# A vector engine's place for splitting weights: before or behind the residual sum of an expert block

## The chip, the cores and the metric

One core of one Trainium2 chip runs the whole program. The metric is the device time of one execution in microseconds; a kernel's time is the median of its runs. The engines are TensorE (PE), VectorE (DVE), ScalarE (ACT), GpSimd (POOL) and SyncE (SP); each works through its own instruction stream in order, and they wait for each other by semaphores.

## The reference

A decoder layer on x of 2048 tokens by 1024 channels, all float32: a norm with conditioning, an RG-LRU token mixer, a second norm, a mixture of 16 experts of width 256 with the two best of one group of four for each token, and a final norm. The part that matters here:

```
x = x + g1[:, None, :] * y
hn = modulate(rmsnorm(x, norm2_g[i]), sh2, sc2)
x = x + g2[:, None, :] * grouped_moe(hn, ...)      # act = silu(hn @ w_gate) * (hn @ w_up) * gate; out = act @ w_down
return rmsnorm(x, final_norm_g)
```

## The kernel before, in words

The program has three stretches: norm and transpose, then the mixer (to about 590 us of the trace), then output projection and routing (to about 820 us), then the experts. Routing writes each token's normed row twice into slots sorted by expert (`hn_slots`), with a record of where its sum is to go, and its residual row (`x_slots`). Slots are cut into blocks of 128 rows; with these inputs there are 39 blocks for 16 experts. Most experts have two or three blocks, one has a single one.

A float32 matmul is made of three passes in a faster format: a value is split into a high half (a rounded copy, made by ScalarE) and a low half (value minus high, made by VectorE), and hi x hi, hi x lo and lo x hi are added. Gate and up weights of an expert are split this way in three parts: part 0 and 1 of 1536 columns, part 2 of 1024. Part 3 is the down weight, which is only copied (2048 columns). SP loads the raw parts; it reloads a raw buffer once the low half (for part 3 the copy) has been made.

The loop over blocks is written out by hand in each engine's stream, with the stages of several blocks interleaved:

- TensorE (`expert_tensor`, L1567), iteration i: `gate_up(i + 2)`, 24 matmuls over eight k; in front of k = 0, 3 and 6 it waits for the low half of part 0, 1 and 2 (L1590). In front of k = 6 and behind that wait it turns the activations of the block before (`turn_act`, L1602, L1605). Then `turn(i + 3)`, the transpose of the gathered rows (L1574), and `down(i + 1)` (L1608, matmuls L1618), which waits for `ah_ready` and for `acc_ready` of the block before.
- ScalarE (`expert_scalar`), iteration i: `load_x(i + 1)` (issues the load of the residual rows, L1400, waits for `acc_ready`), `square(i)` (L1441, waits for the sum of block i), `high_a(i + 1)` (L1412, the activations that `down(i + 1)` needs), `tanh(i + 2)`, `high_x(i + 3)`, `scale_row(i)` (L1432), `high_w(i + 2)` (L1414, copies at L1425).
- VectorE (`expert_vector`, L1494), iteration i: `act_product(i + 2)` (L1505, L1508), `low_x(i + 3)` (L1515), `y_scaled(i + 1)` (L1520, waits for the down of block i + 1), `accumulate(i + 1)` (L1530 copies an index, L1531 makes the sum `e_ab`; they wait for the scatter of the block before, `acc_out`), then the low halves `low_w` (L1288, L1296).
- GpSimd (`expert_gpsimd`), iteration i: `weigh(i)` (L1323, L1325), `scatter_out(i)` (L1313), `scatter_acc(i + 1)` (L1306, writes the sum back to `x_slots`, waits for `acc_ready`), `root(i + 1)` (L1333 to L1341).

Which weights are converted beside which block is in a table, `tab["convert"]`, read by `convert_word` (L1282): beside an expert's first block parts 0 and 1 of the next expert are made, beside its second block part 2 (and ScalarE copies part 3), and beside a block that is its expert's only one all of them. ScalarE's `high_w` waits until the downs of the expert before are done (`d_mm`), since they use the same half of the buffer. `low_w` waits for each high half by `hi_done`:

```
for q in ((0, 1), (2,))[part]:
    dve.wait_ge(w["hi_done"], NQ * e + (q + 1))
```

Of the kernel before, what the change touches and what calls it, by code (L numbers as in the profile page):

```python
# [1217 lines left out]
def experts(nc, ctx, sem, cst, io, tab, w, dr, g2row, out):  # L1218


    if True:
# [60 lines left out]
        def convert_word(eng, b):  # L1282

            v = eng.value_load(tab["convert"][0:1, ds(b, 1)], min_val=128 + 4, max_val=128 * MAXB + 4 * E + 3)
            expert = (v >> 2) & 31
            return ((v >> 1) & 1, v & 1), expert, (expert & 1) * DOWN, v >> 7

        def low_w(dve, word):  # L1288
            dues, e, off, before = word
            for part in range(2):  # L1290
                with dve.If(dues[part] == 1):
                    for q in ((0, 1), (2,))[part]:
                        dve.wait_ge(w["hi_done"], NQ * e + (q + 1))
                        dve.nop(nofuse=True)
                        cols = ds(off + QAT[q], QAT[q + 1] - QAT[q])
                        nc.vector.tensor_tensor(w["lo"][:, cols], raw1[q][:], w["hi"][:, cols].bitcast(F32),  # L1296
                                                ALU.subtract).then_inc(w["lo_done"][q % 2], 1)
# [196 lines left out]
        def expert_vector(dve):  # L1494
            def low_first(q):
                dve.wait_ge(w["hi_done"], q + 1)
                wcols = slice(QAT[q], QAT[q + 1])
                nc.vector.tensor_tensor(w["lo"][:, wcols], raw0[q][:], w["hi"][:, wcols].bitcast(F32),
                                        ALU.subtract).then_inc(w["lo_done"][q % 2], 1)

            def act_product(b):
                if isinstance(b, int) and b == 0:
                    dve.wait_ge(rec_in, 16 * LEAD)
                dve.wait_ge(th_ready, b + 1)
                nc.vector.scalar_tensor_tensor(th[:], th[:], 1.0, gu[:, 0:FE], ALU.add, ALU.mult).then_inc(tmp_ready, 1)  # L1505
                dve.wait_ge(tmp_ready, b + 1)
                dve.nop(nofuse=True)
                nc.vector.scalar_tensor_tensor(av[:], th[:], recs[:].bitcast(F32)[:, ds(b, 1), 2], gu[:, FE:2 * FE],  # L1508
                                               ALU.mult, ALU.mult).then_inc(av_ready, 1)

            def low_x(b):
                for h in range(2):
                    cols = slice(h * HX, (h + 1) * HX)
                    dve.wait_ge(xh_ready, 2 * b + h + 1)
                    nc.vector.tensor_tensor(xl[:, cols], tp[:, cols], xh[:, cols].bitcast(F32), ALU.subtract)\  # L1515
                        .then_inc(xl_ready, 1)

            def y_scaled(b):
                dve.wait_ge(d_mm, b + 1)
                nc.vector.tensor_tensor(pd[:], pd[:], g2row[:], ALU.mult).then_inc(y_ready, 1)  # L1520

            def accumulate(b, first=False):
                dve.wait_ge(y_ready, b + 1)
                dve.wait_ge(xa_in, (b + 1) * 16)
                if not first:
                    dve.wait_ge(squared, b)
                    dve.wait_ge(scaled_row, b)
                    dve.wait_ge(acc_out, b * 16)
                dve.nop(nofuse=True)
                nc.vector.tensor_copy(idx_a[:], recs[:, ds(b, 1), 0]).then_inc(idx_a_ready, 1)  # L1530
                nc.vector.tensor_tensor(ab, pd[:], xa[:], ALU.add).then_inc(acc_ready, 1)  # L1531

            low_x(0)
            low_first(2)
            nless = blocks_less(dve)
            low = lambda b: low_w(dve, convert_word(dve, b))
            act_product(0)
            low_x(1)
            dve.wait_ge(w["lo_done"][0], 2)
            dve.wait_ge(w["hi_done"], NQ)  # L1540
            low(0)
            act_product(1)
            low_x(2)
            y_scaled(0)
            accumulate(0, True)
            low(1)
            for b in range(2):
                act_product(b + 2)
                low_x(b + 3)
                y_scaled(b + 1)  # L1550
                accumulate(b + 1)
                low(b + 2)
            with dve.Fori(2, nless) as i:
                act_product(i + 2)
                low_x(i + 3)
                word = convert_word(dve, i + 2)
                y_scaled(i + 1)
                accumulate(i + 1)
                low_w(dve, word)
            act_product(nless + 2)  # L1560
            y_scaled(nless + 1)
            accumulate(nless + 1)
            low(nless + 2)
            y_scaled(nless + 2)
            accumulate(nless + 2)

        def expert_tensor(pe):  # L1567
# [69 lines left out]
            down(nless + 2)  # L1637

        return expert_sync, expert_scalar, expert_vector, expert_gpsimd, expert_tensor


# [101 lines left out]
```

## Time and profile before

| | us |
|---|---|
| median of 3 runs | 1295.15 |
| lowest, highest | 1294.07, 1295.36 |
| the profiled execution | 1300.12 |
| its span | 1298.5 |
| granted TensorE clock over the span | 0.945 of full |

| engine | busy us | share of the span |
|---|---|---|
| PE | 1097.5 | 85% |
| DVE | 792.0 | 61% |
| ACT | 621.8 | 48% |
| POOL | 632.7 | 49% |

Times in the trace are counted from the start of the span. A line of a timeline has start, duration, engine, source line, operation, output <- inputs, and in brackets the idle time of the engine ahead of it with what ended it. A matmul's end is modelled. PEclk is the mean granted clock of TensorE: 1.00 is 2.4 GHz and 0.50 is 1.2 GHz. "issue" is idle time for which the profile shows no other engine as its cause.

### The profile page before, as it was taken

The page shows a single profiled execution, that of the slowest core. Times are in us where ns is not written, and L with a number is a line of the kernel's source. Part 1 is how long each engine was busy: PE and PEld are TensorE (multiplying, and loading weights), DVE is VectorE, ACT ScalarE, POOL GpSimd, SP SyncE. Part 2 cuts the span into 40 slices and gives each one's busy share as a digit, 9 for nine tenths or more (in the row PEclk, how much of TensorE's full clock was granted, in tenths as well). Part 3 has the DMA queues.
Part 4 walks back from the last instruction along what each step waited for, and adds up shares of the span by engine and source line. Part 5 has one row for each costly group of instructions (what it writes and reads, how often), then busy time and mean ns, then how long its engine had stood idle before and what let it go on. Part 6 is the DMA issues. An engine that isn't in the chain of part 4 may idle for free. (4 is left out here: it accounts for less than half of the span.)

```text
span 1298.5 us, 18937 instructions
## 1 busy us (share of the span) xinstructions
PE 1097.5 (85%) x4704; PEld 837.5 (64%) x4705; DVE 792.0 (61%) x1193; ACT 621.8 (48%) x851; POOL 632.7 (49%) x681
## 2 busy tenths in 40 slices
PE   1358999999999999189999991799789899999991
PEld 0246787787787787178888871576566566666660
DVE  6894557666676684445667768365456555556541
ACT  1464676667667765423222212255555645555541
POOL 0465537246255270012566667055546556656663
PEclk9998999999999999589999995799898999999996
DMA  8445153344334412462354627866677876776741
GB/s 307 162 114 186 52 180 104 111 133 148 98 117 149 130 49 96 180 229 89 133 194 186 225 116 259 276 223 229 224 260 247 276 280 233 249 243 231 247 132 65
DMA packets 142583, 232.55 MB, mean 179 GB/s; under 512 B 32576, under 2 KB 100160, under 8 KB 141904
## 3 DMA queue, kind: packets, MB, share of 16 engines
q1 hardware_dynamic: 101776, 128.10, 29.9%
q0 software_dynamic: 23632, 62.49, 13.5%
q10 hardware_dynamic: 17136, 41.51, 9.9%
q8 instruction: 17, 0.28, 0.1%
q14 instruction: 22, 0.18, 0.0%
HBM read 177.43 MB, written 91.31 MB: 207 GB/s over the span
## 5 line engine op out<-in xcount | busy, mean ns | idle before, releaser
L1618 PE MATMUL po<-w_dn,e_ah 128*128 (+1 forms) x312 | 146.9, 615 | 19.9 <-ACT e_ah L1412 11.9
L1597 PE MATMUL pl<-w_hi,e_xh 128*128 (+1 forms) x312 | 142.8, 458 | 9.6 <-DVE w_lo L1296 5.1
L1165 PE MATMUL po<-wo_hi,b_yh 128*128 128x512 f32 x256 | 105.6, 412 | 27.6 <-DVE wo_lo L979 27.6
L1599 PE MATMUL pl<-w_hi,e_xl 128*128 (+1 forms) x312 | 126.0, 404 | 0.0
L1598 PE MATMUL pl<-w_lo,e_xh 128*128 (+1 forms) x312 | 125.5, 402 | 0.0
L1325 POOL TENSOR_TENSOR e_ob<-e_obs,e_fg 128x1024 f32<-128x1024 f32 x39 | 93.5, 2397 | 56.7 <-ACT e_obs L1432 56.7
L543 DVE SCALAR_TENSOR_TENSOR XB<-xu,conv_w,XB 128x512 f32<-128x512 f32 x96 | 91.4, 952 | 43.0 <-ACT XB L413 39.3
L1618 PEld LDWEIGHTS po<-w_dn,e_ah 128*128 128x128 f32 x312 | 58.4, 197 | 81.4 <-issue 81.4
L636 PE MATMUL px<-hT_hi,wx_hi 128*128 128x512 f32 x256 | 102.0, 398 | 5.1 <-DVE wx_lo L477 5.1
L636 PE MATMUL pg<-hT_hi,wg_hi 128*128 128x512 f32 x256 | 104.2, 407 | 0.0
L1167 PE MATMUL po<-wo_hi,b_yl 128*128 128x512 f32 x256 | 102.3, 400 | 0.0
L1166 PE MATMUL po<-wo_lo,b_yh 128*128 128x512 f32 x256 | 102.1, 399 | 0.0
L637 PE MATMUL px<-hT_lo,wx_hi 128*128 128x512 f32 x256 | 101.8, 398 | 0.0
L638 PE MATMUL px<-hT_hi,wx_lo 128*128 128x512 f32 x256 | 101.8, 398 | 0.0
L638 PE MATMUL pg<-hT_hi,wg_lo 128*128 128x512 f32 x256 | 101.1, 395 | 0.0
L637 PE MATMUL pg<-hT_lo,wg_hi 128*128 128x512 f32 x256 | 101.1, 395 | 0.0
L1441 ACT ACTIVATE e_sq<-e_ab 128x1025 f32<-128x1025 f32 x39 | 41.4, 1062 | 102.3 <-DVE e_ab L1531 95.4
L612 POOL TENSOR_SCALAR macc<-stg,cond 128x512 f32<-128x512 f32 x8 | 11.3, 1407 | 155.3 <-PE pmod L659 149.9
L618 POOL TENSOR_TENSOR macc<-macc,mtmp 128x512 f32<-128x512 f32 x56 | 84.3, 1505 | 4.7
L1597 PEld LDWEIGHTS pl<-w_hi,e_xh 128*128 128x128 f32 x312 | 60.8, 195 | 31.7 <-issue 21.4
L1408 ACT ACTIVATE e_xh<-b_pt 128x512 fp32r<-128x512 f32 x78 | 42.3, 595 | 78.0 <-issue 49.5
L1306 POOL DMA_INDIRECT x_slots<-e_ab,e_idx_a x38 | 44.9, 1183 | 62.6 <-DVE e_ab L1531 55.0
(266 smaller groups left out, 2661.8 us busy)
## 6 DMA issues: line engine op xcount, KB each, us to landing
e_xg<-hn_slots ACTq DMA_DIRECT2D x40, 512.0 KB
e_xa<-x_slots ACTq DMA_DIRECT2D x39, 512.0 KB
stg<-in_ada_w_dram POOLq DMA_DIRECT2D x32, 512.0 KB, 4.2
w_raw<-in_moe_w_down_dram SPq DMA_DIRECT2D x16, 1024.0 KB
w_raw<-in_moe_w_gate_dram SPq DMA_DIRECT2D x32, 384.0 KB
w_raw<-in_moe_w_up_dram SPq DMA_DIRECT2D x32, 384.0 KB
n_ada<-in_ada_w_dram SPq DMA_DIRECT2D x16, 512.0 KB, 5.0
n_x<-in_x_dram SPq DMA_DIRECT2D x16, 512.0 KB, 3.3
```

Of the source, the lines that this page charges most:

```text
L543: nc.vector.scalar_tensor_tensor(xb, xu[:, n, w:w + NB], cw[:, ds(j, 1), w], xb, ALU.mult, ALU.add).then_inc(done, 1)
L636: nc.tensor.matmul(dst[:], whi[br][:, k], hT_hi[:, k, cols], start=(k == 0), stop=False)
L637: nc.tensor.matmul(dst[:], whi[br][:, k], hT_lo[:, k, cols], start=False, stop=False)
L638: last = nc.tensor.matmul(dst[:], wlo[br][:, k], hT_hi[:, k, cols], start=False, stop=(k == KD - 1))
L1165: nc.tensor.matmul(po[u][:, hcols], yh[u][:, tok], wo_hi[:, k, hcols], start=(k == 0), stop=False)
L1166: nc.tensor.matmul(po[u][:, hcols], yh[u][:, tok], wo_lo[:, k, hcols], start=False, stop=False)
L1167: last = nc.tensor.matmul(po[u][:, hcols], yl[u][:, tok], wo_hi[:, k, hcols], start=False, stop=(k == KD - 1))
L1325: nc.gpsimd.tensor_tensor(ob[:], obs[:], fg[:], ALU.mult).then_inc(out_ready, 1)
L1597: nc.tensor.matmul(gu[:], xh[:, tok], hi, start=(k == 0), stop=False)
L1598: nc.tensor.matmul(gu[:], xh[:, tok], lo, start=False, stop=False)
L1599: last = nc.tensor.matmul(gu[:], xl[:, tok], hi, start=False, stop=(k == KD - 1))
L1618: last = nc.tensor.matmul(dst, ah[:, k * P:(k + 1) * P], rows, start=(k == 0), stop=(k == KF - 1))
```

## The change

VectorE's low halves of a block's weights are moved from behind `accumulate` to in front of it, behind `y_scaled`. In the two blocks written out ahead of the loop, in the loop and behind it the order becomes `y_scaled`, low halves, `accumulate`. `low(0)` and `low(1)` keep their places. Nothing else changes; the instructions are the same.

```diff
@@ -1548,19 +1548,19 @@
                 act_product(b + 2)
                 low_x(b + 3)
                 y_scaled(b + 1)
+                low(b + 2)
                 accumulate(b + 1)
-                low(b + 2)
             with dve.Fori(2, nless) as i:
                 act_product(i + 2)
                 low_x(i + 3)
                 word = convert_word(dve, i + 2)
                 y_scaled(i + 1)
+                low_w(dve, word)
                 accumulate(i + 1)
-                low_w(dve, word)
             act_product(nless + 2)
             y_scaled(nless + 1)
+            low(nless + 2)
             accumulate(nless + 1)
-            low(nless + 2)
             y_scaled(nless + 2)
             accumulate(nless + 2)
```

## Rows read from the trace of the kernel before

**Rows 1.** Windows: span, each engine's busy us, PEclk, DMA share, GB/s; the loop
```profile
844.00:1275.00 431.00, 391.90 (x1556) 267.61 (x1554) 237.37 (x304) 229.93 (x319) 250.49 (x303) 0.96 0.69 234
```

**Rows 2.** Waits of PE, 844 to 1275 us: waiting, releaser, total us, times, longest
```profile
PE prank L1605 <- DVE w_lo L1296: 13.9, 6, 3.5
PE po L1618 <- ACT e_ah L1412: 11.9, 4, 5.4
PE po L1618 <- issue: 7.9, 6, 1.8
```

**Rows 3.** Timeline of PE: the first down, two late in the loop, the last
```profile
840.31 3.60 PE L1618 MATMUL po<-w_dn,e_ah 128*128 128x512 f32 x8
...
1240.39 3.60 PE L1618 MATMUL po<-w_dn,e_ah 128*128 x8
...
1250.41 3.60 PE L1618 MATMUL po<-w_dn,e_ah 128*128 x8
...
1269.73 5.15 PE L1618 MATMUL po<-w_dn,e_ah 128*128 x8 [5.41 <-ACT e_ah L1412]
```

**Rows 4.** Groups of DVE by line and shape, 848 to 1275 us: the low halves
```profile
L1296 DVE TENSOR_TENSOR w_lo<-w_raw,w_hi 128x1536 f32 x28 | 47.8, 1750 | 0.1
...
L1296 DVE TENSOR_TENSOR w_lo<-w_raw,w_hi 128x1024 f32 x15 | 18.2, 1216 | 0.4 <-issue 0.4
```

**Rows 5.** Timeline, one step with parts 0 and 1, 1043.94 to 1053.93 us
```profile
1043.94 1.23 DVE L1520 TENSOR_TENSOR po<-po,g2row 128x1024 f32<-128x1024 f32 x1 [0.38 <-PE po L1618]
...
1045.79 1.21 DVE L1531 TENSOR_TENSOR e_ab<-po,e_xa 128x1024 f32<-128x1024 f32 x1
1046.92 3.42 DVE L1296 TENSOR_TENSOR w_lo<-w_raw,w_hi 128x1536 f32 x2
...
1044.34 2.87 ACT L1425 ACTIVATE w_hi<-w_raw 128x1536 f32 x2 [0.58 <-PE po L1618]
...
1050.33 3.60 PE L1618 MATMUL po<-w_dn,e_ah 128*128 x8
```

**Rows 6.** Timeline, the step behind it, from its scatter to its down
```profile
1049.94 1.24 POOL L1306 DMA_INDIRECT x_slots<-e_ab,e_idx_a  x1 [0.30 <-issue]
...
1053.97 1.23 DVE L1520 TENSOR_TENSOR po<-po,g2row 128x1024 f32<-128x1024 f32 x1 [0.28 <-PE po L1618]
1059.39 0.15 DVE L1530 COPY e_idx_a<-e_recs 128x1 int32 x1 [4.19 <-DMA x_slots<-e_ab,e_idx_a]
...
1063.21 5.39 PE L1618 MATMUL po<-w_dn,e_ah 128*128 x8 [2.50 <-ACT e_ah L1412]
```

**Rows 7.** Timeline, one step with part 2, 1177.49 to 1184.98 us
```profile
1177.49 1.23 DVE L1520 TENSOR_TENSOR po<-po,g2row 128x1024 f32<-128x1024 f32 x1 [0.35 <-PE po L1618]
1181.82 0.15 DVE L1530 COPY e_idx_a<-e_recs 128x1 int32 x1 [3.10 <-DMA x_slots<-e_ab,e_idx_a]
...
1183.02 1.22 DVE L1296 TENSOR_TENSOR w_lo<-w_raw,w_hi 128x1024 f32 x1
...
1178.19 1.06 ACT L1425 ACTIVATE w_hi<-w_raw 128x1024 f32 x1 [0.44 <-issue]
...
1184.29 0.69 PE L1605 MATMUL prank<-ident,e_av 128*128 128x128 f32 x2 [2.75 <-DVE w_lo L1296]
```

**Rows 8.** Windows behind two waits of PE (of 3.48 and 2.50 us)
```profile
967.10:970.50 3.40, 3.40 (x18) 2.62 (x19) 0.89 (x2) 1.44 (x4) 2.28 (x6) 1.00 0.90 244
...
1063.21:1068.60 5.39, 5.39 (x9) 2.37 (x10) 2.10 (x4) 2.10 (x3) 3.42 (x6) 0.68 0.89 295
```

**Rows 9.** Timeline of POOL: output scatter without and with low halves on DVE beside it
```profile
1035.10 1.09 POOL L1313 DMA_INDIRECT out_dram<-e_ob,e_idx_o  x1 [0.85 <-issue]
...
1113.63 2.61 POOL L1313 DMA_INDIRECT out_dram<-e_ob,e_idx_o  x1 [0.85 <-DVE e_ab L1531]
```

**Rows 10.** Timeline of PE behind the single-block expert: first matmul and down
```profile
937.11 0.79 PE L1597 MATMUL pl<-w_hi,e_xh 128*128 x1 [5.11 <-DVE w_lo L1296]
...
945.91 3.60 PE L1618 MATMUL po<-w_dn,e_ah 128*128 x8
```

## The prediction

> **What bounds the kernel now.** Read the stages by windows first. The loop over the expert blocks fills 844 to 1275 us; TensorE is busy 391.9 us of 431, VectorE 237 and ScalarE 230 [rows 1]. So TensorE sets the pace, and the question is only what makes it stand. Next, the downs: the first ends at 843.91 and the last, of block 38, at 1274.88, so 38 steps take 430.97 us; two downs late in the loop end 10.02 apart (1243.99, 1254.01), with nothing in front of them [rows 3]. 38 such steps are 380.8 us: **50.2 us are lost**, and no change in VectorE's order can move anything but these. TensorE's waits name their causes [rows 2]: 13.9 us in six pieces for the low halves of a third part of the weights (the wait in front of the turn of the activations), 19.8 us in front of the down, where ScalarE's `ah` is late; one 5.1 us wait is the expert with a single block [rows 10]. Of the 19.8, 6.1 are in the last two steps, which the change does not reach. The rest of the 50.2 is mostly half clock after a wait.
>
> **What is moved.** 28 instructions of 1536 columns and 1750 ns (14 pairs, parts 0 and 1) and 14 of the 15 of 1024 columns and 1216 ns (part 2; the first belongs to `low(1)`, which stays) [rows 4]. Nothing is added or removed; no DMA is issued by the moved code. They go past the copy of `idx_a` and the sum, and who waits for the sum is: POOL's scatter, ScalarE's next load of `xa`, and ScalarE's square, behind which `high_a` is queued, which the next down needs. I count three kinds of step, each from the start of `y_scaled` (Y).
>
> **Kind A, a pair (13 steps, and one with all three parts).** Today [rows 5]: ScalarE starts the two high copies at Y+0.40 (it waits for the same down), both take 2.87, so the first is there at about Y+1.9; the sum runs from Y+1.85 to Y+3.06; the lows from Y+2.98; the next down starts at Y+6.39, when TensorE itself is ready. After the change VectorE ends the scaling at Y+1.23, waits to Y+1.95 for the first high copy, spends 3.34 on the pair (1046.92 to the next start at 1050.26), and the sum runs from about Y+5.4 to Y+6.6. How long the sum's lateness takes to reach TensorE is seen in the very next step [rows 6]: there the last scatter's DMA held `idx_a` to 1059.39, so the sum ran from Y+5.49 to Y+6.71 (0.07 behind the copy and 1.21 long, as in [rows 5]), and the down began 2.53 later, at Y+9.24, after a wait of 2.50. The earliest the sum could begin, were the copies ready, is Y+4.6; the latest, were both copies to finish before the first low, Y+6.7 (waits of TensorE of 2.0 and 4.0). I take Y+5.4, from the copy that each low really waits for. SP, which reloads a raw part once its low is made, gets the word 1.0 earlier, and ScalarE finds the loads landed today. The down then starts at Y+9.1, TensorE waits 2.7, and the slack of 0.8 (6.39 - 3.06 - 2.53) is gone.
> The clock comes on top. In [rows 8] the down of [rows 6] took 5.39 instead of 3.60 at a granted clock of 0.68 (partly 1.2 GHz), while another stretch behind a wait of 3.48 kept 1.00. Eight waits of 2.29 us or more stand in the loop; behind the other six the stretches read 0.50 to 0.68 too. Behind five that I read of 1.4 to 1.9 us it stayed at 1.00. So I take 11 of the 13 with a fall. Such a step is 14.67 long ([rows 3, 6]: the downs end at 1053.93 and 1068.60), 4.65 over; without, 2.7 over. 11 x 4.65 + 2 x 2.7 = 56.6.
> **The expert with one block:** TensorE waits today 5.11 for part 0, and its down begins 8.80 after that [rows 10]. The low of part 0 comes after the scaling and not after the sum, 1.3 earlier: 7.5 over today (17.5 long), 6.2 after.
>
> **Kind B, part 2 alone (13 steps).** Here the change gives. Today [rows 7] the sum waits 3.10 for the last scatter, and the low stands behind both: it starts at 1183.02, 5.5 after Y at 1177.49, and TensorE waits 2.75 for it. High part 2 is there at 1179.25, as the scaling is ending; so after the change the low runs inside the scatter's wait, Y+1.8 to Y+3.0, and TensorE comes for it at about Y+4.0. This wait goes in all six places. What is late next is the sum, by the scatter: it left at 1049.94, 2.94 after its sum, and landed 9.45 later [rows 6]. The 17 for which a sum waited landed 7.3 to 9.8 after they left; I take 8.5, where most of them lie. In kind A after the change the sum ends at Y+6.6, the scatter leaves 0.85 later and lands at Y+16.0. If the clock fell the next step begins at Y+14.7 and the scatter is hidden: 0 over. If not, it begins at Y+12.7, the sum starts at +3.4, and the step is 0.7 over. B and the steps behind it without weights (6): 2 x 0.7 + 6 x 0.5 = 4.4.
>
> **A rule set against a row.** Beside the pair of lows, POOL's issue of the output scatter takes 2.61; with none beside it, 1.09 [rows 9]. The Trainium skill (SBUF — State Buffer, "Summary: rules for kernel authors") has it that when a VectorE instruction has two SBUF inputs and GpSimd's reads SBUF, the second to issue blocks until the first is done; the trace agrees in size. Going by the row alone, the scatters of kind A leave 2.94 behind their sum today and 0.85 after, 2.1 earlier. Were the sum not itself late, that would be 2.1 off the waits for the scatter; it is 3.5 later, so the scatter still leaves 1.4 later, and my sum gives nothing for it.
>
> **The sum.** 56.6 + 6.2 + 4.4 + 0.8 for the last step (10.8 long, as now) = 68.0 lost, against 50.2: **+17.8 us**. The profiled execution took 1300.1 (span 1298.5), 5 above the median of 1295.15; I put the difference on the median, 1312.
>
> **Rivals.**
> 1. *The clock holds in kind A.* 13 x 2.7 + 3.8 + 19 x 0.7 + 0.8 = 53.0: +3, 1298. For it: waits to 1.8 did not cost the clock, one of 3.48 didn't either [rows 8]. Against: seven of eight.
> 2. *TensorE's slack swallows the pair (faster).* What decides is ScalarE: if `ah` did not stand behind the square, the sum could be 3.5 late unseen, and only kind B would count. B and the steps behind it carry about 39 of today's 50.2 (those six waits, those for `ah`, the clock behind them). After: 6.2 + 13 x 0.7 + 3 = 18, so -32, 1263. It turns at a sum that ends by Y+3.9. Its price is real, but [rows 6] shows the chain sum, square, `ah`, down with 2.53 and no slack. The early scatter above would be part of this case.
> 3. *Nothing measurable.* If the first high copy came before the scaling ends, A would lose 2.0 and mostly keep its clock; 13 x 2 + 18 = 44, -6, and with some falls 0: 1295. Against: the copy waits for the same down as the scaling.
> 4. *Each fall of the clock lasts longer.* The longest stretch at half rate behind a wait is some 6 us; 13 x (2.7 + 3.2) + 11 = 88: +37, 1332.
> That the edit does nothing is excluded: VectorE runs in program order and all 42 instructions change place.
>
> **Chances.** Forecast 0.61, rival 1 0.14, rival 2 0.09, rival 3 0.07, rival 4 0.09. Range 1298 to 1326: the forecast, rival 1, part of 4. About 0.2% (2.6 us) is what a measurement can tell from no change: faster 0.10 (rival 2, a little of 3), same 0.09, slower 0.81.
>
> **What the profile after would show.** In kind A: the lows between scaling and sum, 0.7 us idle ahead of them by `w_hi`, the sum ending at Y+6.6, TensorE waiting 2.5 to 2.9 for `ah` 13 times, a wait total in front of the down of about 40 us, and a lower granted clock than 0.96 in the loop. In kind B: no wait of the turn for `w_lo` and hardly a wait of the sum for the scatter. I am wrong if the down in kind A starts near Y+6.4, or if the waits for `w_lo` stay.

## The result, and the profile after

The changed kernel takes **1325.59 us** (five runs, 1316.03 to 1335.69) against 1295.15: 1.023 times as long, 95% interval 1.0191 to 1.0269, **+30.4 us**. Slower is clear of the noise; whether by more than 2% the interval leaves open. The forecast said 1312 (+17), with a range to 1326. The sign and the main mechanism, the late sum behind a pair, came as written; the size was 1.8 times too small, and the median lies 0.4 us under the end of the range. The profiled execution is the slowest of its five (1335.69, span 1334.1, against 1300.12 of the profile before), so its loop overstates the typical loss: where a few us matter below, medians are set against medians.

The first rows to compare are windows over the loop, from the end of the first down (837.21) to the end of the last (1310.44), with the columns of [rows 1]:
```profile
837.00:1310.50 473.50, 414.92 (x1557) 274.25 (x1555) 237.46 (x304) 227.22 (x319) 232.92 (x304) 0.92 0.64 213
```
The instructions are those of [rows 1], but the loop is 473.2 long and not 431.0, TensorE is busy 23 us more for the same work at a clock of 0.92 and not 0.96, and VectorE is busy as long as before. (The first down ended 6.7 us earlier, which takes the loop's +42.3 to the profile's +35.6. The profiles of this study end their first down anywhere from 837 to 847; nothing here rests on that.) What TensorE waited for, and VectorE beside it:
```profile
PE po L1618 <- ACT e_ah L1412: 49.5, 17, 5.8
PE pl L1597 <- DVE w_lo L1296: 4.3, 1, 4.3
PE po L1618 <- issue: 3.0, 3, 1.2
```
```profile
DVE e_idx_a L1530 <- DMA x_slots<-e_ab,e_idx_a: 20.1, 7, 5.2
DVE w_lo L1296 <- ACT w_hi L1425: 13.3, 14, 1.0
```
Against [rows 2], the six waits of the turn for `w_lo` (13.9 us) are gone, and the wait ahead of the down for `ah` went from 11.9 in 4 to 49.5 in 17. VectorE stands 0.95 us 14 times for a high copy, and seven sums still wait for the scatter of the step before.

A step with parts 0 and 1, and the down behind it, against [rows 5]:
```profile
1094.46 1.23 DVE L1520 TENSOR_TENSOR po<-po,g2row 128x1024 f32<-128x1024 f32 x1 [1.40 <-PE po L1618]
...
1096.64 3.45 DVE L1296 TENSOR_TENSOR w_lo<-w_raw,w_hi 128x1536 f32 x2 [0.95 <-ACT w_hi L1425]
1100.01 0.14 DVE L1530 COPY e_idx_a<-e_recs 128x1 int32 x1
1100.08 1.21 DVE L1531 TENSOR_TENSOR e_ab<-po,e_xa 128x1024 f32<-128x1024 f32 x1
...
1102.10 1.06 ACT L1441 ACTIVATE e_sq<-e_ab 128x1025 f32<-128x1025 f32 x1 [4.37 <-DVE e_ab L1531]
...
1103.16 0.36 ACT L1412 ACTIVATE e_ah<-prank 128x256 f32<-128x256 f32 x1
...
1103.82 5.39 PE L1618 MATMUL po<-w_dn,e_ah 128*128 x8 [2.78 <-ACT e_ah L1412]
```
The sum starts at Y+5.62 and not Y+1.85. The square cannot start before the sum, `ah` stands behind the square, and TensorE, ready at Y+6.6, begins its down at Y+9.36 after 2.78 of waiting. The clock then falls, in 12 of the 13 such steps; windows over a down with the fall and over the one without:
```profile
1103.82:1109.21 5.39, 5.39 (x9) 2.37 (x10) 2.10 (x4) 4.50 (x5) 3.45 (x6) 0.68 0.81 265
...
1228.92:1232.62 3.70, 3.70 (x9) 1.79 (x10) 2.10 (x4) 2.81 (x4) 2.12 (x6) 1.00 1.07 390
```
Here is every step of the loop (from the end of one down to the end of the next), in us over 10.02 each (38 x 10.02 = 380.8), by what its VectorE work holds. A is a step with a pair, B one with part 2, C one without weights:

| steps | before | after | forecast |
|---|---|---|---|
| 13 with parts 0 and 1 (A) | 2.6 | 63.2 | 56.6 |
| 14 with part 2 (B), 13 of them moved | 33.4 | 0.2 | 1.4 |
| 8 without weights (C) | 5.9 | **19.1** | 3.0 |
| the single-block expert | 7.5 | 7.0 | 6.2 |
| the last two | 0.8 | 2.9 | 0.8 |
| over the least time | 50.2 | 92.5 | 68.0 |

The surprise is the third line: of the seven such steps behind a moved part 2 (the prediction counted six), five lose 5.7, 6.2, 1.4, 4.3 and 1.5 us.

### The profile page after: what moved, and what is told of

It is laid out like the page before. It is cut to its first block and busy times, and to the rows that moved or that the text cites. A ratio compares the mean times of both kernels' runs of the same rounds, so it can differ in the third digit from the quotient of the medians.

```text
span 1334.1 us, 18937 instructions
## 1 busy us (share of the span) xinstructions
PE 1118.4 (84%) x4704; PEld 842.0 (63%) x4705; DVE 790.8 (59%) x1193; ACT 619.2 (46%) x851; POOL 631.4 (47%) x681
## 5 line engine op out<-in xcount | busy, mean ns | idle before, releaser
L1618 PE MATMUL po<-w_dn,e_ah 128*128 (+1 forms) x312 | 174.0, 710 | 52.6 <-ACT e_ah L1412 49.5
L1618 PEld LDWEIGHTS po<-w_dn,e_ah 128*128 128x128 f32 x312 | 67.7, 228 | 131.9 <-issue 131.9
L1306 POOL DMA_INDIRECT x_slots<-e_ab,e_idx_a x38 | 37.8, 995 | 130.4 <-DVE e_ab L1531 129.2
L1520 DVE TENSOR_TENSOR po<-po,g2row 128x1024 f32<-128x1024 f32 x39 | 48.1, 1233 | 71.1 <-PE po L1618 70.7
```

The source lines that it names most:

```text
L1618: last = nc.tensor.matmul(dst, ah[:, k * P:(k + 1) * P], rows, start=(k == 0), stop=(k == KF - 1))
```

## The experiments

All ratios are to the kernel before on the same chip, whose medians ran from 1292.7 to 1295.6. "Over" is the loop of the profiled execution above 380.8 us.

**1 and 2. Each half of the change alone.** In the first the pair goes ahead of the sum and part 2 stays behind it; in the second part 2 (and all three parts of the single-block expert) goes ahead and the pair stays behind.
```
# 1
 y_scaled(i + 1)
+low_w(dve, word, (0,))    # parts 0 and 1
 accumulate(i + 1)
-low_w(dve, word)
+low_w(dve, word, (1,))    # part 2
# 2
 y_scaled(i + 1)
+low_case(dve, word, AHEAD)    # part 2 alone, or all three
 accumulate(i + 1)
-low_w(dve, word)
+low_case(dve, word, BEHIND)   # parts 0 and 1
```


> Only parts 0 and 1 stand ahead of the sum; part 2 is made behind it, as in the kernel before. Theory 1 (the late sum, through square and ah, holds TensorE in the 13 steps with a pair, 2.8 us of waiting and about 1.8 of half clock each): these steps stay near 14.8 us long, the whole is 20 to 30 us slower than before, close to the changed kernel; TensorE waits about 0.3 to 0.6 us for w_lo in the steps with part 2. Rival A (what costs is that part 2 ahead of the sum starts the reload of the raw weights before the sum's scatter, which then lands in 10 to 12 us): the waits of the sum for the scatter in the steps without weights go from 4 to 6 us back to under 2, and the time is 15 us below the changed kernel.

Measured: 1317.48, ratio 1.0158 (1.0105 to 1.0211). Over 73.2: A 59.2, B 4.6, C 0.4. The steps did what Rival A says as well: C is back at nothing, though the time is 8 us under the changed kernel and not 15.

> Only part 2 (and all three parts of the expert with one block) stands ahead of the sum; the pair of parts 0 and 1 stays behind it. Theory 1: the steps with a pair are 10.03 us long again, TensorE's waits for w_lo at the turn of the activations (13.9 us in the kernel before) are gone; the waits for ah behind a sum held by the scatter stay. Faster than before by 5 to 15 us. Rival A: as part 2 ahead lengthens the scatter, no gain: within 3 us of before or slower.

Measured: 1290.80, ratio 0.9965 (0.9938 to 0.9992), just under the 5 us expected. Over 45.6: A 5.1, B 18.1, C 13.9. The waits of both:
```profile
PE po L1621 <- ACT e_ah L1412: 42.1, 14, 5.8
...
PE prank L1608 <- DVE w_lo L1296: 3.0, 6, 1.4
```
```profile
PE po L1641 <- ACT e_ah L1430: 15.1, 5, 5.4
PE po L1641 <- issue: 15.1, 19, 1.6
...
DVE e_idx_a L1548 <- DMA x_slots<-e_ab,e_idx_a: 30.5, 13, 4.9
```
So the pair is what makes the kernel slower: with it alone it is 22 us slower, with part 2 alone a bare 4 us faster. The rest of the 30 comes only with both. The 19.1 of the C steps need part 2 ahead: put it back and they are 0.4. In the second kernel the `w_lo` waits at the turn are gone, and fewer sums wait for a scatter than before (13 and 30.5 us, against 17 and 46.0), but C loses 13.9 and not 5.9. Something that part 2's early low sets off makes its step's scatter land late. What B still loses there is mostly another matter: 11 of the 13 moved B sums wait for no scatter (experiment 12 has the rows).

**3 and 4. Take `ah` out from behind the square.** The chain sum, square, `ah`, down is cut on ScalarE, in the changed kernel and in the one before.
```
+high_a(i + 1)
 load_x(i + 1, rows[0])
 square(i)
-high_a(i + 1)
```


> The changed kernel, with ScalarE's high_a(i + 1) ahead of load_x(i + 1) and square(i) in its loop, so that the down's input no longer stands behind the sum. The down still waits for the sum itself (acc_ready). Theory 1: in the steps with a pair TensorE waits 0.3 to 0.6 us instead of 2.8, its clock holds, those steps are near 10.5 us; the whole is 35 to 60 us faster than the changed kernel and faster than the kernel before. Rival B (the cost lies in the chain sum, scatter, next sum, or in VectorE's waits for the high copies, 13 us): less than 10 us faster than the changed kernel.

Measured: 1298.23, ratio 1.001 (0.9983 to 1.0036). That is 27 us off the changed kernel, level with before. Over 46.3: A 20.5 (0.9 to 2.1 a step), B and C 16.3. Its waits, and the down of an A step:
```profile
PE po L1618 <- DVE e_ab L1531: 14.1, 15, 1.5
PE po L1618 <- ACT e_ah L1412: 5.8, 1, 5.8
```
```profile
1083.93 3.70 PE L1618 MATMUL po<-w_dn,e_ah 128*128 x8 [1.33 <-DVE e_ab L1531]
```
The wait for `ah` is gone 16 times of 17 and the clock holds (3.70, not 5.39). What is late next is the sum itself: the down writes into the PSUM that the sum still reads, so it cannot begin before that sum ends. The expectation had named this second edge, but priced it at 0.3 to 0.6 us a step; it took 0.6 to 1.5. So the A steps take 11.6 us and not 10.5, and the gain of 27 is short of the 35 expected.

> The kernel before with high_a ahead of load_x and square. Theory 1: the waits for ah behind a sum held by the scatter (13.7 us in the loop) shrink to under 4; the waits for w_lo (19 us) stay. 10 to 20 us faster than before, slower than the changed kernel with the same edit, which has no waits for w_lo. Rival B: no change beyond 3 us.

Measured: 1297.86, ratio 1.0037 (1.0007 to 1.0068): no gain, a miss. In its profile the waits did shrink as expected (for `ah` from 11.9 us in four to 5.4 in one), while the turn still waits for `w_lo` (13.4 us, six times), and the loop is 420.0. But this profiled execution was the fastest of ten and alone would have read as a gain of 11; what takes it back in the other nine no trace shows.

**5 and 6. Let the sum's scatter leave ahead of the output's.** POOL's order is swapped, in the kernel before and on top of experiment 2.
```
 weigh(i)
+scatter_acc(i + 1)
 scatter_out(i)
-scatter_acc(i + 1)
```


> The kernel before, with GpSimd's scatter of the sum ahead of its scatter of the output. If the output scatter, stretched to 2.6 us beside the low halves, is what makes the sum's scatter late behind a pair (it leaves 2.94 us behind the sum in 9 steps), the sum's scatter leaves 0.85 behind the sum everywhere, the sums of the steps with part 2 wait up to 2.1 us less for it, and TensorE's waits for w_lo (13.9 us) and ah fall by half or more: 10 to 20 us faster than before. Rival: the transfer and not its start sets when it lands, since the raw weights' loads are in flight: within 3 us of before.

> Part 2 alone ahead of the sum (the pair behind it), and GpSimd's scatter of the sum ahead of its scatter of the output. If both of the above hold, nearly all of TensorE's waits in the loop go but the one of the expert with one block: 20 to 35 us faster than before, and the fastest so far. If part 2 ahead gives back through a slower scatter what it gains: no better than the kernel with part 2 ahead alone, 5 us under before.

Measured: 1311.18, ratio 1.0116 (1.008 to 1.0151), and 1334.23, ratio 1.0301 (1.0268 to 1.0334). Both went the wrong way. POOL in one step of the first:
```profile
976.66 0.18 POOL L1323 COPY e_idx_o<-e_recs 128x1 int32 x1 [5.11 <-DMA out_dram<-e_ob,e_idx_o]
976.81 2.35 POOL L1325 TENSOR_TENSOR e_ob<-e_obs,e_fg 128x1024 f32<-128x1024 f32 x1
979.34 2.40 POOL L1306 DMA_INDIRECT x_slots<-e_ab,e_idx_a  x1 [0.18 <-POOL e_ob L1325]
982.04 1.24 POOL L1313 DMA_INDIRECT out_dram<-e_ob,e_idx_o  x1 [0.30 <-issue]
```
The output's scatter now leaves last, so the next block's `idx_o` waits 5.11 us for it, and the multiply and the sum's scatter stand behind that wait (133.6 us in 35 such waits over this loop, 21.0 in the kernel before). The queue moved past was POOL's own, and what stood behind it was not counted. These two say nothing about the C steps.

**7. Keep TensorE's clock up through the wait.** 22 transposes of the identity into an unused PSUM bank ahead of the down of each A step; the kernel's own work is unchanged.
```
 turn(i + 3)
+filler(i + 1)      # where parts 0 and 1 are due: 22 transposes
 down(i + 1)
```


> The changed kernel, with 22 transposes of a constant into an unused bank on TensorE ahead of the down of the step that follows a pair, so that it works through the wait for ah instead of standing. They take no input of the computation and give it nothing. If the clock that falls behind the wait is the second cost of these steps (2.05 us each beside 2.7 us of waiting), they go from 14.8 to 12.8 us and the whole is 20 to 28 us faster than the changed kernel, with no wait of TensorE removed. If the long downs have another cause, the steps stay at 14.8 or get longer.

Measured: 1315.09, ratio 1.013 (1.0066 to 1.0193), 10.5 us off the changed kernel at the medians, where 20 to 28 were expected. A lost 40.2 and not 63.2.
```profile
1098.12 2.56 PE L1572 MATMUL po<-ident 128*128 128x128 f32 x22
1101.09 3.69 PE L1624 MATMUL po<-w_dn,e_ah 128*128 x8 [0.40 <-issue]
```
An A step loses 3.06 and not 4.75, and the down takes 3.69: of the 4.75, 1.7 was the clock and the rest the lateness itself. In the profiled loops A gives 23 us, at the medians the whole gives half that. Of the difference, 8.4 us stand in front of the loop (the first down ends at 845.6 and not 837.2), and the two profiled executions are 10.1 and 6.0 above their medians. The four executions run from 1306.9 to 1321.1, so the 10.5 is rough.

**8 and 9. Hold back the reload of part 2.** Part 2's low frees its raw buffer, on which SP starts the next expert's part 2 and, behind it, its down weights. Here SP also waits for a semaphore, which VectorE raises behind the sum (8) or, later, behind the next activation product (9).
```
 sp.wait_ge(w["lo_done"][q % 2], (2 * e - 1, e, 2 * e)[q])
+if q == 2:
+    sp.wait_ge(raw2_free, e - 1)
...
 accumulate(i + 1)
+release(dve, word)     # 8: a nop that raises raw2_free
...
 act_product(i + 2)
+free(dve, i + 1)       # 9: the same nop, here and not there
```


> The changed kernel, with SyncE's reload of the raw buffers of part 2 and of the down weights held back until VectorE has made the sum behind part 2. If these loads, which now start about 1 us ahead of the sum's scatter, are what makes it land after 9.5 to 12 us instead of 8.5, the waits of the steps without weights (19 us over the least time in the changed kernel) fall under 6 us, and the whole is 10 to 16 us faster than the changed kernel. Rival: the sum of a step with part 2 simply follows the late sum of the pair too closely; then nothing changes within 4 us.

Measured: 1334.35, ratio 1.0282 (1.0237 to 1.0327). Over 87.8, C 19.4: no change, and the profile says why the edit did not test its claim:
```profile
883.96 1.22 DVE L1538 TENSOR_TENSOR e_ab<-po,e_xa 128x1024 f32<-128x1024 f32 x1
...
884.01 0.37 SPq L702 DMA_DIRECT2D w_raw<-in_moe_w_gate_dram  x1
...
886.01 0.97 POOL L1313 DMA_INDIRECT x_slots<-e_ab,e_idx_a  x1 [2.85 <-DVE e_ab L1538]
```
The nop let SP go 0.05 us after the sum had begun, not after it had ended, and 2.0 ahead of the scatter. The Trainium skill (VectorE: DVE Perf Modes, "Two Vector instructions with no wait between them") says that a nop is handled by the sequencer alone; that agrees with the 0.05.

> The changed kernel again with SyncE's reload of part 2 and the down weights held, now until VectorE has come to the next block's activation product, some 2 us after the sum's scatter is issued. In the run before this the hold was let go as the sum was issued and not when it ended, so that the loads started at 884.01, 2.0 us ahead of the scatter at 886.01, as without it. If the loads ahead of the scatter are what makes it land after 9.5 to 12 us, its last packet now ends 6 to 8 us after the issue in the steps with part 2 (10.2 to 11.0 in the changed kernel), the steps without weights lose under 6 us in all instead of 19, and the whole is 10 to 16 us faster than the changed kernel. Rival: it does not depend on the loads; then the scatter stays at 10 to 11 us.

Measured: 1314.60, ratio 1.0138 (1.0095 to 1.0181), 11.0 us off the changed kernel at the medians. Over 69.8: A 60.3, B 0.6, **C 0.1**. Same place, changed kernel first, then this one:
```profile
874.10 1.21 DVE L1531 TENSOR_TENSOR e_ab<-po,e_xa 128x1024 f32<-128x1024 f32 x1
...
874.14 0.37 SPq L702 DMA_DIRECT2D w_raw<-in_moe_w_gate_dram  x1
874.55 0.47 SPq L703 DMA_DIRECT2D w_raw<-in_moe_w_up_dram  x1
875.07 0.47 SPq L698 DMA_DIRECT2D w_raw<-in_moe_w_down_dram  x1
...
876.14 0.98 POOL L1306 DMA_INDIRECT x_slots<-e_ab,e_idx_a  x1 [2.63 <-DVE e_ab L1531]
...
888.23 0.15 DVE L1530 COPY e_idx_a<-e_recs 128x1 int32 x1 [5.18 <-DMA x_slots<-e_ab,e_idx_a]
```
```profile
882.62 0.97 POOL L1314 DMA_INDIRECT x_slots<-e_ab,e_idx_a  x1 [2.83 <-DVE e_ab L1539]
...
886.39 0.37 SPq L702 DMA_DIRECT2D w_raw<-in_moe_w_gate_dram  x1
...
889.99 0.15 DVE L1538 COPY e_idx_a<-e_recs 128x1 int32 x1 [0.47 <-DVE po L1528]
```
With the weight loads 2.0 ahead of it, the scatter kept the next sum waiting until 12.1 us after its issue; with the loads 3.8 behind it, it kept nobody waiting 7.4 after its issue. The DMA view of the 5 us from the scatter's issue (queue, packets, MB, share of the 16 DMA engines; q1 and q10 carry loads, q0 POOL's scatters), changed kernel first:
```profile
q1 hardware_dynamic: 478, 0.99, 76.6%
q10 hardware_dynamic: 46, 0.19, 17.1%
```
```profile
q10 hardware_dynamic: 255, 0.98, 58.7%
q0 software_dynamic: 144, 0.52, 25.9%
...
x_slots<-e_ab,e_idx_a POOLq DMA_INDIRECT x1, 4.1
```
In 5 us the changed kernel moves not one packet of the scatter, and the held one all 144; it landed in 4.1. The packets of q0, counted off 144 to a scatter in order, give the same for all 12 B steps with a reload: in the changed kernel the first packet starts 4.6 to 5.4 us after the issue and the last ends after 7.2 to 11.0; here it is 1.8 to 2.3 and 2.6 to 4.3. So the C losses are the scatter behind 1.5 MB of weight loads; that is shown by moving only the loads.

**10 to 12. Towards a faster version.** 10 is experiment 2 with the edit of 3; 11 is 10 with the hold of 9; 12 is experiment 2 with the hold of 9 and ScalarE's order as before.

> Part 2 ahead of the sum, the pair behind it, and ScalarE's high_a ahead of the load of the residual rows and the square. No wait for w_lo at the turn, and a sum held by the scatter costs only what it exceeds Y+6.4 by: TensorE's loop is 395 to 405 us long (431 before), 15 to 30 us faster than before. Rival (the load of xa and the square, now later on ScalarE, make the residual's own chain the bound, as in the two kernels with high_a first that stayed level with before): within 5 us of before.

Measured: 1298.81, ratio 1.0034 (1.0003 to 1.0065), a miss. With `ah` early, ScalarE's next split of `x` comes late, and the first matmuls of a block wait for VectorE's `e_xl` (15.7 us in 21 pieces, none in experiment 2).

> The kernel of the run beside it, with the reload of part 2 and the down weights held as well. If both views are right it is the fastest: 2 to 8 us below the one without the hold, since the sums wait less for the scatter. Rival: once high_a stands first the scatter's landing is off TensorE's path, and the hold changes nothing within 3 us or costs a little where raw weights come late.

> Part 2 ahead of the sum, the pair behind it, the reload of part 2 and the down weights held until the next activation product, and ScalarE's order as before. The kernel with part 2 ahead alone lost 32 us in the steps without a pair, where its sum waited for the scatter to Y+3.2 to Y+6.3 and the down followed. If the scatter lands in 4 to 6 us behind part 2, as in the held run, these steps lose under 12 us, the loop is 400 to 410 us (431 before) and the whole is 12 to 25 us faster than before, the fastest of all. Rival: the steps behind a pair keep a scatter of 7.5 us and more that leaves late beside the low halves, and the gain stays at 5 to 10 us, level with the kernel that has high_a first.

Measured: 1285.87, ratio 0.9938 (0.9916 to 0.996), and **1284.93**, ratio 0.9932 (0.9909 to 0.9955; before beside it 1292.66). Both beat either kernel, the one before by 0.6 to 0.7%; between them nothing can be told. Over 36.4 in the last: A 0.5, C 0.5 (13.9 without the hold), B 27.3. I had expected 12 to 25 us from it and got 7.7, the size that the rival gave. Where the rest stays:
```profile
PE po L1654 <- issue: 12.9, 12, 2.1
PE po L1654 <- ACT e_ah L1438: 10.1, 3, 5.3
```
The sums of the 13 moved B steps start at Y+3.4 to Y+5.3, not Y+1.8, and two things hold them. In three steps, which lose 13.2 of the 27.3, it is the scatter of the A step before, which lands 8.8 to 9.4 us after its issue. That this is again loads (of parts 0 and 1, whose raw buffers the pair frees, and which here start 1.2 us ahead of that scatter) was not tried. In nine of the ten others the sum follows the low half with no wait that the profile shows, and in the tenth after 0.15: there the low half of part 2 is itself late, long or both. One such step, VectorE with GpSimd beside it:
```profile
975.68 2.41 POOL L1351 TENSOR_TENSOR e_ob<-e_obs,e_fg 128x1024 f32<-128x1024 f32 x1 [1.52 <-ACT e_obs L1458]
...
976.91 2.27 DVE L1304 TENSOR_TENSOR w_lo<-w_raw,w_hi 128x1024 f32 x1
...
979.10 0.14 DVE L1556 COPY e_idx_a<-e_recs 128x1 int32 x1
979.17 1.21 DVE L1557 TENSOR_TENSOR e_ab<-po,e_xa 128x1024 f32<-128x1024 f32 x1
```
Where GpSimd's multiply `e_ob` runs beside it, this low takes 1.7 to 2.8 us (12 of the 13 steps) and ends about 1.1 after the multiply; with next to none of it beside, as in the 13 moved B steps of the changed kernel, it takes 1.2 to 1.3. So moving part 2 ahead of the sum puts this stretched instruction in front of the sum, and the expectations of 10 and 12, which gave these waits to the scatter alone, missed it. No run moves the multiply to test it.

## Why the prediction was right in sign and short in size

1. **What moves, and that it is the pair that costs.** Right. Taking the pair alone ahead costs 22 us, part 2 alone gives 4.
2. **Kind A, the sum's start.** Y+5.4 was taken, inside 4.6 to 6.7; measured Y+5.59 to Y+6.11. The first 0.2 are the first high copy, which came at Y+2.18 and not Y+1.95. The four late ones (5.80 to 6.11) have a first low of 1.96 to 2.09 us and not 1.76 (in them GpSimd's multiply ends at Y+2.5 or later, in the others by Y+2.3), and one of them a wait for a scatter of 0.19 as well. The chain of 2.53 from [rows 6] held exactly (1101.29 to 1103.82), and the down at Y+9.1 came at Y+9.4. Experiment 3 shows the chain by cutting it.
3. **Kind A, the clock.** 11 falls of 13 were taken, 12 came, and twice the down took 6.5 to 6.7 us and not 5.4. A typical step lost 4.75 against the 4.65 of [rows 3, 6]. 56.6 became 63.2: a term too small by a tenth. Experiment 7 puts 1.7 of each step on the clock, which is the difference of 5.39 and 3.69, and [rows 8] had it right. How often it falls is less certain than 12 of 13 looks: behind the same waits in experiments 1, 8 and 9 it held in 3, 4 and 4 of 13.
4. **Kind B.** Right: the low ran inside the time in which the sum had waited, all six turn waits went, 0.2 lost against 1.4 forecast.
5. **The step that failed: the scatter's landing of 8.5 us, and with it 6 x 0.5 for the steps behind part 2.** It was read from scatters of the kernel before, where part 2's low stood behind the sum and its reload mostly started 0.3 us behind the scatter, and it was carried over to an order where the reload starts 2.0 ahead of it. The text did say that SP "gets the word 1.0 earlier", for the pair, and stopped there; for part 2, where the low is ahead of the sum by its own 1.2 and the scatter leaves 0.8 behind the sum, the same thought gives loads in front of the scatter. In the five C steps that lost time it had landed after 9.5 to 12 us, and 3.0 became 19.1, of which experiment 9 gives back all. The kernel before held the warning: in two of its B steps POOL sent the sum's scatter late, 1.2 us behind the loads, and those two landed after 9.8 and 9.5 us, the top of the range of 7.3 to 9.8. The second of them, from three views:
```profile
1013.52 0.37 SPq L702 DMA_DIRECT2D w_raw<-in_moe_w_gate_dram  x1
...
1014.76 0.98 POOL L1306 DMA_INDIRECT x_slots<-e_ab,e_idx_a  x1 [0.30 <-issue]
...
1024.30 0.15 DVE L1530 COPY e_idx_a<-e_recs 128x1 int32 x1 [3.35 <-DMA x_slots<-e_ab,e_idx_a]
```
6. **The single block** lost 7.0, not 6.2, and the last two steps 2.9, not 0.8. Small, and not pursued.
7. **The rule set against a row.** In the B steps the output scatters now leave ahead of the low; in nine of the 13 A steps they still lie beside the pair and take 1.7 to 2.2 us. Their group on POOL:
```profile
L1313 POOL DMA_INDIRECT out_dram<-e_ob,e_idx_o x38 | 48.3, 1271 | 33.4 <-issue 29.1 <-DVE e_ab L1531 2.6 <-DVE e_idx_a L1530 0.8
```
   They average 1271 ns, against 1512 ns for the 37 before, between the two durations of [rows 9]. The sum's scatter leaves 0.8 behind the sum, as the text had it. The reverse, a low half held by GpSimd's multiply, the text did not have; in this kernel it costs only the 0.2 to 0.3 us of point 2, four times.
8. **The sum.** Missing against the profile (+42.3 in the loop, forecast +17.8): 6.6 in A, 16.1 in C, 2.9 in the last two and the single block, less 1.2 in B, which is 24.4 of 24.5. Profile against profile the time missed 17.8, since the first down ended 6.7 earlier; at the medians 12.7, since the profiled execution of the changed kernel ran 10.1 over its median and that of the kernel before 5.0; the 1312 of the forecast is the sum of 1313 (1295.15 + 17.8) put 1 too low, which makes it 13.6.
9. **The range.** That 1325.59 lies inside 1298 to 1326 is partly luck: its upper part was there for falls of the clock that last longer, and it was mostly filled by the C steps, for which the prediction had no rival.

The rivals: that slack swallows the pair is out (13 waits of about 2.8); that the clock holds is out (it fell in 12 of 13); and falls that last longer were seen twice in 13, so the 1332 of that case was near for another reason.

Still open: why the five executions of the changed kernel spread over 20 us. The profile shows only the slowest, but the granted clock of each is known and runs against the time: 0.933 in the slowest, then 0.940, 0.941 and 0.946, and 0.949 in the fastest. That fits waits that are followed by a fall in one execution and not in the next; what decides it is not shown.

## What to carry to other kernels

Moving an instruction ahead of another on one engine moves the transfers that it sets free as well: list what each moved instruction releases, on which queue, and what small transfer then starts behind it. When an operation is made late, follow it through the in-order queue of the *next* engine, where an innocent neighbour (here `ah` behind the square) may carry the delay to the engine that bounds the kernel. A duration of a DMA read from a trace is the duration beside the traffic of that order; when the order changes, bound it anew. And ask which instruction of another engine will run beside the moved one in its new place: it may take longer there.

## What the runs showed of the hardware that was not expected

- A scatter of 128 rows from POOL, issued 2.0 us behind 1.5 MB of weight loads on SP's queue, sent its first packet 4.6 to 5.4 us after its issue and ended after 7.2 to 11.0; with the loads 3.4 to 4.0 us behind it, 1.8 to 2.3 and 2.6 to 4.3 (12 steps each). The start suffers, not only the rate.
- A nop on VectorE placed behind a sum raised its semaphore 0.05 us after the sum's start, 1.17 before its end.
- Waits of TensorE of some 2.6 to 3.1 us were followed by a fall of the granted clock (0.68 over the next down in the one shown) in 12 of 13 steps of the changed kernel; in experiment 3, where the longest of the 15 such waits was 1.5, 37 of the loop's 38 downs took 3.59 to 3.70. Behind the same waits in experiments 1, 8 and 9, the down took the 3.7 us of the full clock in 3, 4 and 4 of 13. With transposes in the wait, the down ran at 1.00.
- A subtraction of 1024 columns on VectorE took 1.2 us alone and 1.7 to 2.8 beside GpSimd's multiply of 1024 columns (experiment 12); it ended about 1.1 after the multiply.
- The same `ah` edit was worth 27 us in one kernel and nothing in the other.
